# Adding two squares on VectorE ahead of the ones-matmul of an RMS norm

## The reference

```python
def rmsnorm(x, g):
    y = xf * lax.rsqrt(jnp.mean(xf * xf, axis=-1, keepdims=True) + EPS)
    return y.astype(x.dtype) * g

for l in range(DEPTH):                      # DEPTH = 2
    mix = hybrid_mixer(rmsnorm(h, norm_mix_pre[l]), ...)
    h = h + rmsnorm(mix, norm_mix_post[l])
    ff = squared_relu_mlp(rmsnorm(h, norm_mlp_pre[l]), w_mlp_up[l], w_mlp_down[l])
    h = h + rmsnorm(ff, norm_mlp_post[l])
return h[:, N_META:]
```

## Time and profile before

| what | us |
|---|---|
| median of 3 runs | 2711.59 (2703.58 to 2718.34) |
| the profiled execution, its time | 2703.58 |
| its span | 2701.8 |
| TensorE matmul busy | 2531.1 (94%) |
| weight load busy | 2403.3 (89%) |
| VectorE busy | 1106.2 (41%) |
| ScalarE busy | 671.1 (25%) |
| GpSimd busy | 1233.2 (46%) |

### The profile page before, as it was taken

The page is one execution under the profiler, slowest core; times in us unless marked ns, Lnnn a source line. Parts: engine busy times, 40 slices in busy tenths (PEclk is TensorE's granted clock), DMA queues, the critical chain, the costliest instruction groups (busy, mean ns, idle before and its releaser), DMA issues.

```text
span 2701.8 us, 37879 instructions
## 1 busy us (share of the span) xinstructions
PE 2531.1 (94%) x15192; PEld 2403.3 (89%) x15192; DVE 1106.2 (41%) x917; ACT 671.1 (25%) x757; POOL 1233.2 (46%) x571
## 2 busy tenths in 40 slices
PE   6779899989999999999978798999899999999998
PEld 5778887978999999999868788779799999999996
DVE  3686543264123222221486773432722123222225
ACT  3444126233000100010245432261501000100015
POOL 6443530464544454444564354206644544454441
PEclk9898996999999999999989889889999999999998
DMA  4100100132111111111141011001411111111113
GB/s 168 43 31 24 39 32 1 47 114 69 48 47 47 43 42 47 47 62 47 55 132 32 24 32 39 24 17 47 142 40 47 47 47 47 45 40 47 62 47 112
DMA packets 60918, 143.36 MB, mean 53 GB/s; under 512 B 5136, under 2 KB 36112, under 8 KB 60816
## 3 DMA queue, kind: packets, MB, share of 16 engines
q1 hardware_dynamic: 28368, 99.20, 11.2%
q10 hardware_dynamic: 32448, 42.77, 5.1%
HBM read 120.57 MB, written 21.38 MB: 53 GB/s over the span
## 4 chain that ended last, share of the span: by engine, by line
PE 77%; DVE 12%; issue 7%; ACT 2%; DVEq 0%; POOL 0%; DMA 0%; ACTq 0%; SPq 0%; POOLq 0%
PE banks L400 66%; PE banks L664 3%; DVE Y L1071 2%; DVE xc L1151 2%; DVE Y L1066 1%; DVE act_lo L1362 1%; PE banks L426 1%; PE banks L636 1%; PE banks L562 1%; DVE xc L1147 1%; PE banks L627 1%; DVE li L1114 1%; PE banks L450 1%; PE banks L722 1%; PE banks L439 1%
## 5 line engine op out<-in xcount | busy, mean ns | idle before, releaser
L400 PE MATMUL banks<-X,w_hl 128*128 128x348 f32 (+1 forms) x7920 | 1289.9, 324 | 20.0 <-DVE k L1020 16.5
L400 PEld LDWEIGHTS banks<-X,w_hl 128*128 128x128 f32 x7920 | 1267.8, 189 | 28.9 <-DVE k L1020 17.1
L325 POOL TENSOR_TENSOR w_hl<-w_raw,par 128x1024 fp32r<-128x1024 f32 x180 | 350.5, 1947 | 1249.9 <-PE banks L400 1246.9
L400 PE MATMUL banks<-act_hi,w_hl 128*128 128x348 f32 x3024 | 567.9, 321 | 5.8 <-DVE act_lo L1362 5.8
L400 PEld LDWEIGHTS banks<-act_hi,w_hl 128*128 128x128 f32 x3024 | 493.9, 188 | 10.4 <-DVE act_lo L1362 10.4
L327 POOL TENSOR_TENSOR w_hl<-w_raw,w_hl 128x1024 fp32r<-128x1024 f32 x180 | 496.6, 2759 | 14.1
L992 ACT ACTIVATE T<-T 128x1044 f32<-128x1044 f32 x64 | 69.0, 1077 | 1205.4 <-DVE T L1357 1205.4
L400 PE MATMUL banks<-act_lo,w_hl 128*128 128x348 f32 x1512 | 321.3, 321 | 0.0
L1357 DVE SCALAR_TENSOR_TENSOR T<-banks,rs 128x1044 f32<-128x1044 f32 x64 | 79.5, 1245 | 563.0 <-PE banks L400 550.8
L1378 DVE TENSOR_TENSOR Y<-banks,Y 128x1044 f32<-128x1044 f32 x96 | 119.6, 1246 | 372.8 <-PE banks L400 372.8
L400 PEld LDWEIGHTS banks<-act_lo,w_hl 128*128 128x128 f32 x1512 | 253.9, 188 | 0.0
(11 more groups left out here) (180 smaller groups left out, 2108.4 us busy)
## 6 DMA issues: line engine op xcount, KB each, us to landing
w_raw<-w_units SPq DMA_DIRECT2D x184, 512.0 KB, 3.3
h_old<-h_out ACTq DMA_DIRECT2D x24, 348.0 KB, 3.7
h_mid<-Y ACTq DMA_DIRECT2D x24, 348.0 KB, 4.1
h_old<-h_mid ACTq DMA_DIRECT2D x24, 348.0 KB, 3.6
h_out<-Y ACTq DMA_DIRECT2D x24, 348.0 KB, 4.1
Y<-x_in ACTq DMA_DIRECT2D x6, 696.0 KB, 9.6
h_out<-Y ACTq DMA_DIRECT2D x6, 696.0 KB, 3.7
gates_raw<-w_gates SPq DMA_DIRECT2D x8, 256.0 KB, 2.6
```

The costliest lines, as they stand in the source:

```text
L325: nc.gpsimd.tensor_tensor(slot[:, 0], w_raw[:, s], gains(l, P_ONE), ALU.mult).then_inc(w_scaled, 1)
L400: ins = nc.tensor.matmul(out[:, b, 0:width(b)], wp, xp[:, used(b)], start=first and n == 0, stop=last and n == 2)
```

## The change

TensorE's two ones-matmuls of a piece become one. VectorE adds the second tile's squares onto the first's in place (`add_pair`), and TensorE waits for that add (`sq_pair`) instead of for ScalarE's square (`sq_h`). In `update` the add of piece n-1 is queued behind the two L1071 of piece n, and that of piece 11 behind everything. In the start stage all 12 adds are queued behind the table's operations. TensorE's wait for banks_zeroed at the start of its program is dropped.

```diff
@@
                 if first:
                     take_sum_bank(l, norm, b)
-                pe.wait_ge(sq_h, sbase + n + 1)
-                nc.tensor.matmul(sum_bank(norm, b), ones[:, :], sq[:, n % SQ_RING, 0, :], start=first, stop=False)
-                nc.tensor.matmul(sum_bank(norm, b), ones[:, :], sq[:, n % SQ_RING, 1, :], start=False, stop=last)\
+                pe.wait_ge(sq_pair, sbase + n + 1)
+                nc.tensor.matmul(sum_bank(norm, b), ones[:, :], sq[:, n % SQ_RING, 0, :], start=first, stop=last)\
                     .then_inc(sum_done if last else sq_read, 1)
@@
             pe.wait_ge(const_ready, 1)
-            pe.wait_ge(banks_zeroed, 2)
@@
+            def add_pair(total, n):
+
+                dve.wait_ge(sq_h, total + n + 1)
+                V.tensor_tensor(sq[:, n % SQ_RING, 0, :], sq[:, n % SQ_RING, 0, :], sq[:, n % SQ_RING, 1, :], ALU.add)\
+                    .then_inc(sq_pair, 1)
@@
                     ins.then_inc(y_new, 1)
+                    if n >= 1:
+                        add_pair(total + NX, n - 1)
+                add_pair(total + NX, NX - 1)
@@
             V.tensor_scalar(nsp, sp, -1.0, None, ALU.mult).then_inc(par_ready, 1)
+            for n in range(NX):
+                add_pair(0, n)
```

More of the change, by code:

```diff
@@ L210, in trunk_kernel @@
         x_hi, x_lo = sem("x_hi"), sem("x_lo")
+        sq_pair = sem("sq_pair")
         sq_h, sq_read = sem("sq_h"), sem("sq_read")
```

## The result

The changed kernel takes 2729.94 us (median of 18 runs, 2720.18 to 2756.0) where the kernel before takes 2711.68 (18 runs, 2700.06 to 2726.46): the ratio is 1.0082, with a 95% interval of 1.0058 to 1.0105. It is slower by about 20 us. The forecast was 2731. The profiled execution after has a span of 2725.6 us, 23.8 more than before.

A forecast was written before the change was run, and what follows sets the result against it. TensorE was taken to bound the start stage, VectorE and GpSimd taking turns the update stages. Start +3.8, updates +13.8 and last +3.0 made 20.6 us; on the 2711.6 median, 2731 us, own range 2724 to 2741, whole 2708 to 2752.

The forecast's parts named there:

- What bounds the kernel: TensorE bounds the start stage; in the update stages VectorE and GpSimd, taking turns without a gap, set the 3.33 us period.
- The removed passes and the dropped wait: 60 ones-matmuls, 34.8 us of TensorE work, count only where TensorE is the bound; dropping the banks_zeroed wait gains nothing.
- Three update stages: Middle stages: nothing hides the add, period 3.33 to 3.78 us, no gain at the end; 3 x 4.6 = +13.8 us.
- the price of one add in a period: Update stages: each VectorE add lengthens the period by 0.45 us, within bounds of 0.44 and 0.51.
- small overlaps: Update stages: VectorE's 0.87 + 1.07 us and GpSimd's 1.65 fill the 3.33 us period, less these.
- Start stage: Adds queued behind the table make TensorE 8.5 us late, later pieces give some back; net +3.8 us, bounds 1 and 7.
- The wait for add 9: Start stage, last pieces: add 9 waits for GpSimd's operation to end, about 1.2 us after TensorE wants the sum.
- Last stage: End of kernel, no GpSimd: period 1.90 to 2.35 us, add 1 waits for its square; net +3.0 us, bounds 1 and 5.
- The sum: All five stages: 3.8 + 13.8 + 3.0 = 20.6 us added to the kernel before.
- TensorE as the pace of all stages: Rival, all stages: 48 pieces save 0.58 us each against the first stall of 8.5; 2692 us, chance 0.04.
- Hidden adds: Rival, middle stages: adds fit in VectorE's time behind GpSimd, only start and end cost, +6.8; 2718 us, chance 0.12.
- The falling clock: Rival, update stages: idle TensorE drops to its low clock, a piece costs 5.0 us, 40 more; 2771 us, chance 0.08.

The follow-up runs named there:

- fp32r run: Squares and ones in fp32r with no add, one pass per ones-matmul, against the kernel before: 2703.4 us, ratio 0.9971.

## Why the prediction was right, point by point

*What bounds the kernel.* Confirmed. The fp32r run takes nearly all sum work from TensorE: 8.7 us come back in the start stage, 3.1 in the last, nothing in the update stages.

*The removed passes and the dropped wait.* They counted only where I said. TensorE's first matmul starts at 15.19 us, and at 15.17 in the kernel before, so the wait for banks_zeroed was worth nothing. In the start stage pieces 2 to 7 are 2.5 us apart, as forecast.

*Three update stages: +13.8 forecast, +9.7 measured* (2.8, 3.3 and 2.9, and 0.7 in all up to the last Ln). The mechanism held: no cover, no wait ahead of the add, TensorE idle behind it. The term that was too large is the price of one add in a period, 0.45. It is 0.29 (3.64 against 3.35). The prediction's own rows had the room: 0.87 + 1.07 + 1.65 is 3.59 us in a period of 3.33, and it passed over the 0.26 as "small overlaps". In the changed kernel the same count, with the add's 0.51, is 4.13 us in a period of 3.64, so the overlaps grew to 0.49. What changed is where GpSimd gets in: L339 is now issued while the scaling runs, waits about 0.2 us (1.87 us where it takes 1.69 unhindered) and goes ahead of both L1076. I read the smaller price from this order; no run sets it apart. The first 0.14 us of an add costs 0.10 (period 3.45), the remaining 0.36 cost 0.19, and a second operation costs 0.56: its whole 0.44 and, as I take it, the wait for its semaphore.

The rule cited in the prediction, of the Trainium skill, "SBUF — State Buffer", section "SBUF: two separate sides", was borne out by this case's traces: an add issued during L339 took 1.43 us and ended 0.37 us behind it, and a scaling that met GpSimd's add took 1.60 instead of 0.87.

*Start stage: +3.8 forecast, +6.6 and +8.0 measured in the two traces of the changed kernel.* The stall was as worked out: first sum at 31.3 forecast, 31.2 measured. The steps that failed are the ones after it. I let pieces 0 and 1 give back 0.5 us; they took 0.6 more (7.83 us from the first sum to that of piece 2, where it was 7.23), with passes of double length through the hi passes of piece 1 (2.32 us for eight). I let pieces 9 to 11 give back 0.5; they cost 1.1 more, with the clock at 0.50 from 57.6 to 61.0 us. The wait for add 9 itself came as worked out: 1.24 us against 1.2. Two other runs have the same instructions up to here, those with the add moved in the update stages: there the last Ln came at 61.8 and 62.1, so +3.6 and +3.9. In the first of them TensorE was idle ahead of piece 9 and its add for the same 1.34 and 1.24 us, and its clock stayed at 1.00. So these idle times alone do not explain the fall, and that two runs land on my +3.8 goes with a clock that rose sooner at the restart and stayed up. The stage's cost is a spread from 3.6 to 8.0.

*Last stage: +3.0 forecast, +3.4 measured* (+4.0 by the second trace of before). The period is 2.34 as forecast and add 1 waits for its square, 0.61 us. What the sum lacked was a term for TensorE's clock. Over the whole stage it is 0.57 in the changed kernel and 0.78 in the kernel before (the 0.80 of the earlier trace rows ends with the last L1071). Before, it was at 1.00 from 2684 to 2697 us; in the changed kernel it is at 0.50 from 2697 to the end. The sum missed only behind the copy of piece 8: up to there the stage grew by 2.4 us (2.55 forecast), from there to the end by 1.1 (0.4 forecast). The last sum takes 1.53 us of it, where at the high level after a wait it takes 0.85; my estimate from these is that the clock makes up the missing 0.7. The windows of before, then of the changed kernel, and two rows of its timeline:

```profile
2671.10:2701.80 30.70, 22.40 (x51) 11.58 (x50) 22.43 (x37) 24.87 (x36) 0.00 (x0) 0.78 0.74 244
...
2684.00:2697.00 13.00, 8.64 (x27) 4.35 (x26) 10.41 (x18) 11.22 (x18) 0.00 (x0) 1.00 0.96 329
```

```profile
2697.00:2725.60 28.60, 17.41 (x24) 5.50 (x22) 22.89 (x40) 20.28 (x29) 0.00 (x0) 0.50 0.79 247
```

```profile
2698.64 0.52 DVE L1018 TENSOR_TENSOR sq<-sq 128x348 f32<-128x348 f32 x1 [0.61 <-ACT sq L777]
...
2722.17 3.14 PE L440 MATMUL banks<-sq,ones 128*128 128x348 f32 x4 [0.81 <-DVE sq L1018]
```

*The sum.* 20.6 forecast, 19.8 from the stages: the update stages were set 4 us too high and the start stage 3 to 4 too low, and the two errors nearly cancel. The medians differ by 18.3, the ratio makes it 22 (16 to 28). So 2731 against 2729.94 is closer than the working deserves: part of it is luck.

*The rivals.* TensorE as the pace of all stages: refuted by the fp32r run. Hidden adds: refuted by the two runs that moved the add. The falling clock: it did not pull the update stages down as that rival had it (0.89, 0.86 and 0.89 of full, against 0.88, 0.91 and 0.88). It did fall once inside one of them, the second, at its last pieces, from 1399.0 to 1402.4 us in the line below, where TensorE was not the bound; and it was low in parts of the start stage and the last.

```profile
1399.00:1402.40 3.40, 3.24 (x11) 2.56 (x11) 2.54 (x3) 1.25 (x2) 1.64 (x2) 0.50 0.26 93
```

Left open: why the clock in the mixers falls for a different time in each execution (about 106 to 151 us in the first mixer over the four traces of the two kernels). The range of the runs, 26 us before and 36 after, goes with the clock: the runs of the changed kernel with a mean granted clock of 0.945 or 0.946 took 2720 to 2728 us, those with 0.931 or 0.932 took 2755 to 2756. The count of executions with a trace is too small to say whether the change moves it.

## What to carry to other kernels

Read the chain of waits for each stretch that an edit touches: an engine that is busy for 94% of the span was not the bound in three of the five stretches in which its work was cut, and in a fourth, the last, at its end at most. Where VectorE and GpSimd already take turns, as here, price an operation moved to VectorE at its whole duration until a run says less: the first add of 0.51 us cost 0.29 a period, a second one 0.56. An idle gap of the trace helps only if the operation stands in it and the gap isn't itself a wait for the shared resource. When work on a busy engine must shrink, look first for a cheaper form on the same engine: here fp32r for the sums, which gained 0.3% where the add lost 0.8%, at the price of rounded squares.

## What the runs showed of the hardware that was not expected

Less work for TensorE did not always mean less time, by its clock. In the last stage the granted clock was 0.78 with two sums a piece (0.83 in the second trace) and 0.57 with one. The sums of the last two pieces took 4.3 us for eight passes before (from 2697.28 us on), and 3.14 for four after. The fp32r run, with still less to do, had 0.57 there too. And one program's two mixers took 1030 us in one execution and 1050 in another with the other engines' busy times equal to within 1 us, at a granted clock of 0.89 and 0.90 against 0.86 and 0.88. Last, small operations stand behind GpSimd as long as large ones: the table's of 128x16 took 1.6 us while L339 ran and 0.17 when it had ended.
